# Three projections as products of rounded and rest parts, and an earlier request for the scan's second operands

## The reference

```
x_r, x_w, x_k, x_v, x_a, x_g = h + xx * mix[0..5]
w[d] = w0[d] + tanh(x_w @ w1[d]) @ w2[d]       # decays, two directions
a[d] = sigmoid(a0[d] + (x_a @ a1[d]) @ a2[d])  # rates
k = x_k @ wk;  kk = k * k_k / |k * k_k| per head of 64
v = x_v @ wv;  r = x_r @ wr
g = sigmoid(x_g @ g1) @ g2
# kk, kk*a[d], k*(1+(a[d]-1)*ka), w[d], r, v go into a state scan, forwards and backwards
```

## Time and profile before

| | us |
|---|---|
| median of three runs (3556.89 to 3564.07) | 3558.8 |
| the profiled execution, its own time | 3566.02 |
| span of its trace | 3564.2 |
| TensorE busy, share of the span | 3320.4, 93% |
| VectorE busy | 1465.2, 41% |
| ScalarE busy | 1168.5, 33% |
| GpSimd busy | 345.6, 10% |

### The profile page before, as it was taken

The page is one execution under the profiler, slowest core; times in us unless marked ns, Lnnn a source line. Parts: engine busy times, 40 slices in busy tenths (PEclk is TensorE's granted clock), DMA queues, the critical chain, the costliest instruction groups (busy, mean ns, idle before and its releaser), DMA issues.

```text
span 3564.2 us, 64276 instructions
## 1 busy us (share of the span) xinstructions
PE 3320.4 (93%) x28608; PEld 2195.6 (62%) x28608; DVE 1465.2 (41%) x2533; ACT 1168.5 (33%) x2226; POOL 345.6 (10%) x283
## 2 busy tenths in 40 slices
PE   6999999999899889988988888899999999999998
PEld 4665444435457488887333332468788876878886
DVE  2352000024651278876420001367743446774343
ACT  3331111113451377765120001345331324533131
POOL 0010000000200255453010000020000001000000
PEclk9999999999899999999989999999999999999999
DMA  8259999985543443433379999621423202142320
GB/s 345 94 210 360 390 377 382 376 338 197 176 172 118 99 92 81 101 78 109 135 301 421 421 408 421 243 67 43 142 95 95 95 30 67 54 142 94 94 84 24
DMA packets 342436, 674.80 MB, mean 189 GB/s; under 512 B 157048, under 2 KB 250744, under 8 KB 286864
## 3 DMA queue, kind: packets, MB, share of 16 engines
q1 hardware_dynamic: 330272, 633.14, 49.3%
q0 software_dynamic: 5264, 18.68, 1.5%
q10 hardware_dynamic: 6624, 18.88, 1.4%
HBM read 636.04 MB, written 34.60 MB: 188 GB/s over the span
## 4 chain that ended last, share of the span: by engine, by line
PE 79%; DVE 9%; DMA 7%; ACT 2%; issue 1%; POOL 0%; SPq 0%; DVEq 0%; ACTq 0%; POOLq 0%
PE ps L1134 15%; PE ps L1145 5%; DMA ring<-in_moe_wu 4%; PE ps L641 3%; PE ps L3485 3%; PE ps L3484 3%; PE ps L3483 3%; PE ps L642 3%; PE ps L643 3%; PE ps L3501 3%; PE ps L3502 3%; PE ps L3500 3%; PE ps L1656 2%; PE ps L1681 2%; PE ps L2367 2%; DMA ring<-in_moe_wg 2%
## 5 line engine op out<-in xcount | busy, mean ns | idle before, releaser
L1134 PE MATMUL ps<-ring,H 128*64 128x512 f32 x2016 | 480.7, 601 | 40.0 <-DMA ring<-in_moe_wu 31.1
L1266 DVE TENSOR_TENSOR scr<-ps,scr 128x512 f32<-128x512 f32 x32 | 22.1, 692 | 885.4 <-PE ps L1134 885.4
L1134 PEld LDWEIGHTS ps<-ring,H 128*64 128x64 f32 x2016 | 148.2, 137 | 326.9 <-issue 242.4
L1134 PE MATMUL ps<-ring,scr 128*64 128x512 f32 x1016 | 245.6, 602 | 29.8 <-DMA ring<-in_moe_wd 25.8
L3465 DVE TENSOR_TENSOR ring_rounded<-ring,scr_rounded 128x2048 fp32r<-128x2048 f32 x64 | 146.7, 2292 | 216.6 <-ACT scr_rounded L3458 216.3
L3500 PE MATMUL ps<-scr_rounded,ring_rounded 128*128 128x512 f32 x512 | 201.8, 394 | 1.6 <-DVE ring_rounded L3465 1.6
L3483 PE MATMUL ps<-scr_rounded,ring_rounded 128*128 128x512 f32 x512 | 202.8, 396 | 0.0
L3485 PE MATMUL ps<-scr_rounded 128*128 128x512 f32 x512 | 202.6, 396 | 0.0
L3502 PE MATMUL ps<-scr_rounded 128*128 128x512 f32 x512 | 202.4, 395 | 0.0
L3484 PE MATMUL ps<-H_rounded,scr_rounded 128*128 128x512 f32 x512 | 202.3, 395 | 0.0
L3458 ACT ACTIVATE scr_rounded<-ring 128x2048 fp32r<-128x2048 f32 x64 | 122.2, 1909 | 242.7 <-PE ps L3502 242.7
(11 more groups left out here) (552 smaller groups left out, 6949.6 us busy)
## 6 DMA issues: line engine op xcount, KB each, us to landing
ring<-in_moe_wu SPq DMA_DIRECT2D x128, 1024.0 KB, 9.8
ring<-in_moe_wd SPq DMA_DIRECT2D x127, 1024.0 KB, 10.4
ring<-in_moe_wg SPq DMA_DIRECT2D x124, 1024.0 KB, 10.5
ring<-in_mlp_w SPq DMA_DIRECT2D x64, 1024.0 KB, 5.3
ring<-in_ada_w SPq DMA_DIRECT2D x48, 1024.0 KB, 9.6
ring<-in_w_in SPq DMA_DIRECT2D x14, 1024.0 KB, 5.3
ring<-in_w_out SPq DMA_DIRECT2D x8, 1024.0 KB, 5.3
st_lw<-scr POOLq DMA_DIRECT2D x16, 384.0 KB, 4.1
```

The lines of the kernel that those rows point to most:

```text
L1134: ins = pe.matmul(bx[64 * n:64 * n + 64, :], stat_x(k), w[:, k % 4, :], start=k == 0, stop=k == KT - 1)
```

## The change

The projections k, v and r are made by `three`. Each of their twelve weights is split by ScalarE and VectorE; each of the three mixed inputs is copied rounded by ScalarE (`high`) into ring slots `xh`, and VectorE leaves the rest in XJ (`rest`). The first two tiles of k and r, and the six token tiles of the first value weight, are made in one pass over k; the others one after the other. The plan of the ring has the second slots, and the gate weights come ahead of wr.1. EXP_AFTER goes from 2 to 4. `wkv_first_loads` is cut in two: its first part (the operands of step 0) stands before wr.3, its second (`wkv_next_loads`) before hold.0, and requests the operands of step 1 behind the stored receptance, before the values and gates. In return ScalarE's evictions of the second step wait for the stored gates.

```diff
 LASTS = {f"i{l}.hh.{n}": f"i{l}.z.1" for l in range(2) for n in range(2)}
 LASTS["yh"] = "i0.ckv"
 LASTS["router0"] = "fwo.3.hi"
+LASTS["router1"] = "wo.3"
+LASTS["a2"] = "wk.3.hi"
+LASTS["g1"] = "hold.0"
+LASTS["g2"] = "hold.0"
+MIXED = {2: ("wk", 3), 3: ("wv", 3), 0: ("wr", 2)}
+for j, (w, n) in MIXED.items():
+    for i in range(n):
+        LASTS[f"xh{j}.{i}"] = w + ".3.hi"
 
 
 def weight_plan(a):
...
-    cols("wk", a["rw_wk"][0])
-    cols("wv", a["rw_wv"][0])
-    cols("wr", a["rw_wr"][0])
-    plan.append(("g1", a["rw_g1"][0]))
-    plan.append(("g2", a["rw_g2"][0]))
+    for j, src in ((2, a["rw_wk"][0]), (3, a["rw_wv"][0]), (0, a["rw_wr"][0])):
+        name, slots = MIXED[j]
+        for i in range(4):
+            split(f"{name}.{i}", src[:, 256 * i:256 * i + 256])
+            for n in range(slots) if i == 0 else ():
+                plan.append((f"xh{j}.{n}", None))
+            if j == 0 and i == 0:
+                plan.append(("g1", a["rw_g1"][0]))
+                plan.append(("g2", a["rw_g2"][0]))
...
+        with nc.sbuf_tensor("before_mix", [P, 6144], F32):
+            with nc.sbuf_tensor("mix", [P, KT, TA], F32) as XJ:
+                pass
...
+        def stream_loads(sp, step):
+            for u, d, c, img, first in step:
+                if later(sp, f"til{u - 2}"):
+                    sp.wait_ge(*at(f"til{u - 2}"))
+                for i, s, h in chunk_streams(d, img):
+                    did(f"ld{d}", sp.dma_start(LD[h, d, i, :].rearrange("p (k t) -> p k t", t=CH),
+                                               dram[s][h, :, c * CH:c * CH + CH]).then_inc(sems[f"ld{d}"], 16), by=16)
+                marks[f"ld{u}"] = (f"ld{d}", count[f"ld{d}"])
...
+        def wkv_next_loads(sp):
+            steps = list(units())
+            for m in range(4, KT):
+                if later(sp, f"s.r.{m}"):
+                    sp.wait_ge(*at(f"s.r.{m}"))
+            stream_loads(sp, steps[1])
             if later(sp, "lg.0"):
...
-            for n in range(1, len(steps)):
+            for n in range(2, len(steps)):
+                stream_loads(sp, steps[n])
...
-        EXP_AFTER = 2
+        EXP_AFTER = 4
+        XJ_r = S(6144, KT, TA, of=scr_r)
+
+        def mixed_high(j, k, s0, sn):
+
+            if s0 < TX:
+                o = TX * (k % 4) + s0
+                return ring_r[:, place[f"xh{j}.{k // 4}"][0], o:o + sn]
+            return ring_r[:, place[f"xh{j}.2"][0], TC * k + s0 - TX:TC * k + s0 - TX + sn]
+
+        def mixed(j, k, s0, sn):
+            return mixed_high(j, k, s0, sn), XJ_r[:, k, s0:s0 + sn]
...
+            def columns(tag, j, parts):
+                wn, slots = MIXED[j]
+                w = split_weight(pe, f"{wn}.{parts[0][0] // 2}")
+                banks = [bank(pe, f"{tag}.{m}.{s0}") for m, s0, sn in parts]
+                for k in range(KT):
+                    if later(pe, f"xlo{j}.{k}"):
+                        pe.wait_ge(*at(f"xlo{j}.{k}"))
+                    for b, (m, s0, sn) in zip(banks, parts):
+                        ins = three(pe, b[:, 0:sn], [t[:, k, (m % 2) * P:(m % 2) * P + P] for t in w],
+                                    mixed(j, k, s0, sn), k == 0, k == KT - 1)
+                        if k == KT - 1:
+                            did(T_, ins.then_inc(tensor_done, 1), f"{tag}.{m}.{s0}")
+                if parts[-1][0] % 2:
+                    marks[f"wf.{wn}.{parts[-1][0] // 2}"] = (T_, count[T_])
...
+            columns("k", 2, [(m, s0, sn) for m in range(2) for s0, sn in SEGS])
+            rates(0)
+            head_norm(0)
+            rates(1)
+            for m in range(2, KT):
+                columns("k", 2, [(m, *SEGS[0])])
+                head_norm(m - 1)
+                columns("k", 2, [(m, *SEGS[1])])
+                if m == KT - 1:
+                    mixed_read(2)
+                rates(m)
...
+                w = split_weight(pe, f"wv.{n}")
+                for tts in [range(TA // P)] if n == 0 else [[tt] for tt in range(TA // P)]:
+                    banks = [bank(pe, f"v.{n}.{tt}") for tt in tts]
                     for k in range(KT):
-                        if later(pe, f"xj3.{k}"):
-                            pe.wait_ge(*at(f"xj3.{k}"))
-                        ins = pe.matmul(b[:, 0:256], XJ[:, k, tt * P:tt * P + P], w[:, k, :], start=k == 0, stop=k == KT - 1)
-                    did(T_, ins.then_inc(tensor_done, 1), f"v.{n}.{tt}")
+                        if later(pe, f"xlo3.{k}"):
+                            pe.wait_ge(*at(f"xlo3.{k}"))
+                        for b, tt in zip(banks, tts):
...
+            columns("r", 0, [(0, 0, TX), (1, 0, TX)])
+            for m in range(2, KT):
+                columns("r", 0, [(m, 0, TX)])
+            mixed_read(0)
...
+            def rest(j, k):
+                if later(dve, f"xhi{j}.{k}"):
+                    dve.wait_ge(*at(f"xhi{j}.{k}"))
+                for s0, sn in SEGS if j else XSEG:
+                    did(V, dve.tensor_tensor(XJ_r[:, k, s0:s0 + sn], XJ[:, k, s0:s0 + sn], mixed_high(j, k, s0, sn).bitcast(F32),
+                                             ALU.subtract).then_inc(vector_done, 1))
+                marks[f"xlo{j}.{k}"] = (V, count[V])
+
+            def parts_of_mix(n):
+                for k in range(KT):
+                    mix(n, (k,))
+                    if k:
+                        rest(order[n], k - 1)
+                rest(order[n], KT - 1)
...
-            mix(2)
+            split_low(dve, "wk.0")
+            parts_of_mix(2)
             for m in range(KT):
                 if m == KT - 1:
-                    mix(3)
+                    parts_of_mix(3)
...
-            mix(4)
+                if m % 2 == 0:
+                    split_low(dve, f"wk.{m // 2 + 1}" if m < KT - 2 else "wv.0")
+            for name in ("wv.1", "wv.2", "wv.3", "wr.0"):
+                split_low(dve, name)
+            parts_of_mix(4)
+            split_low(dve, "wr.1")
             mix(5)
+            split_low(dve, "wr.2")
...
                 chunk_tildes(dve, *un)
+            split_low(dve, "wr.3")
             chunk_begin(dve, *first_step[0])
...
+            def high(j):
+                for k in range(KT):
+                    if later(act, f"xj{j}.{k}"):
+                        act.wait_ge(*at(f"xj{j}.{k}"))
+                    if k % 4 == 0:
+                        slot_free(act, f"xh{j}.{k // 4}")
+                    if k == 0 and j:
+                        slot_free(act, f"xh{j}.2")
+                    for s0, sn in SEGS if j else XSEG:
+                        did(A_, act.activation(mixed_high(j, k, s0, sn), XJ[:, k, s0:s0 + sn], ACT.Copy).then_inc(scalar_done, 1))
+                    marks[f"xhi{j}.{k}"] = (A_, count[A_])
+            split_high(act, "wk.0")
             lora("la", 1, ACT.Copy, SEGS)
+            high(2)
...
+                if m % 2 == 0:
+                    split_high(act, f"wk.{m // 2 + 1}" if m < KT - 2 else "wv.0")
+                if m == KT - 1:
+                    high(3)
...
+                if tag == "r":
+                    high(0)
+                    split_high(act, "wr.1")
...
+                    if tag == "v" and m in (0, 3, 5, 7):
+                        split_high(act, {0: "wv.1", 3: "wv.2", 5: "wv.3", 7: "wr.0"}[m])
...
+                    if tag == "r" and m in (1, 3):
+                        split_high(act, f"wr.{m // 2 + 2}")
...
+            for m in range(4, KT) if u == 2 else ():
+                if later(act, f"s.g.{m}"):
+                    act.wait_ge(*at(f"s.g.{m}"))
...
+                if name == "wr.3":
+                    wkv_first_loads(sp)
                 if name == "hold.0":
-                    wkv_first_loads(sp)
+                    wkv_next_loads(sp)
```

More of the change, by code:

```diff
@@ L393, in wkv_first_loads @@
                 sp.wait_ge(*at(f"xj5.{KT - 1}"))
-            steps = list(units())
-            for u, d, c, img, first in steps[0]:
+            for u, d, c, img, first in next(units()):
                 for n, s, h in chunk_streams(d, False):
@@ L1593, in build @@
         XX = S(0, KT, TA)
-        XJ = S(6144, KT, TA)
         ST = [S(12288 + TA * n, TA) for n in range(10)]
@@ L1646, in head_norm @@
                     did(T_, pe.matmul(b[:, 0:sn], bones[:, :], SQ[:, s0:s0 + sn], start=True, stop=True).then_inc(tensor_done, 1), f"kn.{m}.{s0}")
[L1647 to L1657, removed]
-                    did(T_, ins.then_inc(tensor_done, 1), f"k.{m}.{s0}")
-                if m % 2:
-                    marks[f"wf.wk.{m // 2}"] = (T_, count[T_])
-                if m == KT - 1:
-                    marks["xjfree2"] = (T_, count[T_])
-                if later(pe, "free.la.0"):
-                    pe.wait_ge(*at("free.la.0"))
-                if later(pe, "free.la.512"):
-                    pe.wait_ge(*at("free.la.512"))
+            def columns(tag, j, parts):
[12 more added lines that the diff above has]
+                    marks[f"wf.{wn}.{parts[-1][0] // 2}"] = (T_, count[T_])
```

(23 more changed lines are left out.)

6 lines of the change are left out of this document (removed).

## The result

The changed kernel takes 3584.7 us (median of 4 runs, 3581.4 to 3587.1) against 3561.3 us for the kernel before beside it (4 runs, 3556.9 to 3564.1): 0.6% slower, ratio 1.006, 95% interval 1.0047 to 1.0073. The forecast was 3567 in a range of 3545 to 3582. Slower was its likeliest direction, and that came. The size did not: +23 us instead of +8, 2.7 us above the range. The profiled execution of the changed kernel spans 3585.3 us, 21.1 more than the one before.

A forecast was written before the change was run, and what follows sets the result against it. TensorE bounds the kernel now, but a ScalarE and VectorE loop takes over in the keys. Terms 9.6 + 2.9 - 13 = -0.5, plus 8 for gaps, give about +8 us: 3574 profiled, median 3567, range 3545 to 3582.

The forecast's parts named there:

- the sum of -0.5: Whole kernel: values +9.6, receptance +2.9 and scan -13 us, before the extra cost of gaps.
- Products: Key, value and receptance products: three rounded ones take 0.68 or 0.36 us, gaining 40 us if TensorE stays the bound.
- Keys, the first rest: Start of the keys: the mix can start at 946.5 and the first rest is there 3.1 us later.
- C: Keys: the time when the first two tiles' single pass over k is done, forecast at 966.3.
- Keys, the loop: Key tiles: the ScalarE and VectorE loop sets the pace, odd tiles 12.6 us, even tiles 13.8.
- Values: Value products: wv.1's split waits behind tile 7's stores, its rest comes at 1097.3, values end 9.6 us later.
- Receptance: Receptance products: wr.3's rest is late, at 48.0, so they end at 59.0 against 56.1 us, +2.9.
- Scan: Scan start: the early request removes VectorE's wait for a load, -13 us.
- What the gaps cost besides their length: TensorE's new gaps: half clock 4 us at long ones, 3 in the keys, late stores 1; together +8, bounds 0 and 16.
- the sum at +11: Whole kernel, if every gap is paid in full at the throttled clock, with 6 us for the keys.
- the third: Rival, more queues: odd key tiles wait for stores, wr.3 lands later, clock lost at each gap; +20 us, 3579; chance 0.12.
- The first: Rival, products set the pace: -45 us, 3514; half of it, about -20, 3539; together chance 0.20.

The follow-up runs named there:

- Experiment 4: Changed kernel with wk.1 split before the first key tile and wk.2, wk.3, wv.0 one tile earlier; 3575.1 us, ratio 1.0027.
- Experiment 2: Changed kernel with ScalarE copying wv.1 before, not behind, the wait for the last key tile's stores; 3572.4 us, ratio 1.0017.
- 12.5 alone: Kernel before with only the early request of the next scan step's operands and ScalarE's new wait for the gate stores; 3550.7 us.
- Experiment 9: Changed kernel with extra unused products filling TensorE's two long gaps, before wv.1's products and receptance tile 6; 3579.0 us.
- Experiment 5: Changed kernel with VectorE making wr.3's rest before the scan's first sums and tildes, SyncE's order unchanged; 3573.7 us, ratio 1.0023.
- experiment 6: Changed kernel with key weights split a tile earlier, wv.1 copied before the store wait, wr.3 requested and split before the first scan loads; 3545.5 us, ratio 0.9937.
- experiment 8: Changed kernel with early key splits, early wv.1 copy, wr.3 ahead of the scan loads, and key stores issued by GpSimd; 3540.6 us, ratio 0.9926.

## Why the prediction was wrong in size

The miss is 21.6 us of profiled time (+21.1 against the sum of -0.5), for which the prediction allowed 8. Step by step:

- **Products**: right. Three are 0.68 us at 512 columns and 0.36 at 256, and the first pass was limited by them. That the loop would take over from them, so that their 40 us would not be gained, was right too.
- **Keys, the first rest**: 949.65, forecast 949.6. C was 968.0 instead of 966.3: the first products ran at 0.43 us, at a half clock that the step had not priced.
- **Keys, the loop**: this is the first step that failed. "From there the loop: odd tiles 12.6" leaves TensorE out of the loop. TensorE was idle on wk.2's rest until 1008.59, as the step says; but it then ran a slow first tile, so the norms and the root of the odd tile came 1.6 to 1.7 us later than VectorE wanted them in tiles 1 and 3. Odd tiles took 44.3 us instead of 37.8. Stores had a share: the last tile's landed 1.2 and 1.8 us behind the usual start of tiles 3 and 5 (forecast: 1 us for all). Experiment 4 took the rests out and found 12.6 and 13.7.
- **Values**: the mechanism was right, wv.1's split behind tile 7's stores. It came at 1107.4 instead of 1097.3, late by what the keys had lost. The value products behind it took 54.3 instead of 51.8 us, at half clock first. Experiment 2 shows that this order alone cost 9.4, and that a wait of 3.3 for the same stores remains in the evictions.
- **Receptance**: +9.4 instead of +2.9. wr.3 was requested 31.4 us after V (29.2 forecast), landed 7.7 us later (6.3) and had its rest at 51.4 (48.0): 3.4. The clock made the other 3.1.
- **Scan**: -13 held: 12.3 in the changed kernel, 12.5 alone.
- **"What the gaps cost besides their length"** is the step that put the sum off. It stood at +8. In its place: 8.0 in the keys (1.7 in the first pass, 6.3 in the loop) where it had 3 for the clock and 1 for the stores, 5.6 behind the two long gaps where it had 4, 3.4 for wr.3's lateness where it had none, 2.8 of small differences on the way (values and scan) and 1.8 behind U (less than that part moves by itself). Together 21.6. The upper bound for this term was 16.

Experiment 9 shows the clock's share at the long gaps directly, 2.7 and 2.8 us. In the keys it was not taken apart from the wait itself: experiment 4 removes both, so how the 6.3 us divide is open. An estimate from the timeline: the 24 products of 512 columns ahead of the norms of tiles 1, 3 and 5 took 7.0, 8.2 and 7.2 us, and those ahead of the norm of tile 2 took 5.7; at the full clock the late stores would still have held tiles 3 and 5 by 1.2 and 1.8 us, so the clock alone made some 3 of the 6.3.

The prediction weighed the rule of the Trainium skill that the throttled state is the default and activity releases it ("TensorE: Matmul & The Clock Gate", What's actually happening), by which it had the sum at +11, not +8. The changed kernel's trace sides with it: half clock stood behind waits of 3.2, 4.8, 3.9, 3.9, 9.6, 13.9, 2.3 and 13.8 us, and in experiment 9 not where filler took the place of the two long ones. Other traces don't bear out that every gap pays: waits of 2.3 and 3.0 us passed at a granted clock of 1.00, as the last section shows.

The other rule, strictly first in, first out on VectorE (the Trainium skill, "TensorE: Matmul & The Clock Gate", Architectural detail), agrees with the trace: the rest of wr.3 began at 1210.81 with its operand ready at 1202.66, though VectorE stood idle for 2.5 us of the time in between, until the exponentials were there that the instruction at the head of its list needed:

```profile
1205.12 0.69 DVE L2212 SCALAR_TENSOR_TENSOR X<-H,scr 128x512 f32<-128x512 f32 x1 [12.35 <-ACT scr L2155]
```

Experiment 5 moved the rest and gained 10.6.

Of the rivals, the third (3579) came nearest, by the same ingredients: odd tiles late, wr.3 late, clock lost at every gap. It was given 0.12. The first, 3539 for "loop as computed, but wv.1 and wr.3 on time", is near what experiment 6 measured, 3545.5, when the order allowed it. The rest of the miss is in the step from profile to median: the forecast took 7.2 off its profiled time, and the changed kernel's median is 2.4 below its own profiled execution.

## What to carry to other kernels

When a product is made cheaper by splitting its operands, ask of every split when it is made, not how long it takes: here the same instructions made the kernel 23 us slower, or 19 faster (14 of them from the early request), by standing behind or ahead of store waits, tildes and a queue of loads. When the engine that sets the time gets gaps, price each long one (14 us here) at its length plus some 3 us of lost clock, and go through the loop again with the slow restart in it. And when one wait on a store is taken away, look for what else stands behind the same stores: here it was the evictions.

## What was not expected of the hardware

- Length of the idle time alone did not decide the clock. In experiment 8 TensorE waited 3.01 us before 1090.55 and ran on at 1.00, as the busy times by stretch show; in the changed kernel 3.23 us before 949.79 were followed by 0.65 on average:

```profile
1090.50:1094.50 4.00, 3.95 (x33) 3.95 (x34) 0.00 (x0) 2.73 (x9) 1.66 (x3) 1.00 0.43 144
```

```profile
949.80:954.00 4.20, 4.20 (x15) 3.57 (x16) 4.20 (x7) 1.88 (x4) 0.00 (x0) 0.65 0.00 0
```

The same wait even went both ways. TensorE waited 2.3 us at the start of the receptance in both kernels; in the changed one 0.50 followed (products from 1164.00), in "wv.1 early" 1.00 (products from 1146.80):

```profile
1165.00:1167.50 2.50, 2.50 (x7) 1.94 (x6) 2.50 (x5) 1.23 (x3) 0.00 (x0) 0.50 1.02 362
```

```profile
1145.00:1150.00 5.00, 3.20 (x14) 2.67 (x15) 4.97 (x9) 2.64 (x5) 0.76 (x1) 1.00 0.76 254
```

- Five stores of 384 KB each, issued together by ScalarE at a tile's end, landed 10.4 to 11.5 us after the first issue in tile 7 of eight kernels, the one before among them, and 6.3 in one (the filler) that has the same loads and stores in its program there. From GpSimd it was 10.5 to 10.8 in three.
- GpSimd issued the five in 2.7 us (1.07 for two), ScalarE in 2.3 to 4.6. By the medians a store landed 0.3 to 0.4 us later from GpSimd's queue, except those of kd in the kernel before (none).
- The stretch ahead of the changed code ended anywhere from 940.4 to 950.0 us in the nine kernels that are the same up to there. Differences of 10 us between two single executions mean nothing until they are placed in a stage.
